# Order of the three split products: term by term across output tiles, with FFN gate and up chunks in pairs (two-block transformer, one Trainium2 core)

## Chip, core and metric

The program runs on 1 core of one Trainium2 chip. The metric is device time in microseconds (us), the median of several executions. The engines are TensorE (PE, matrix products; its weight load is listed as PEld), VectorE (DVE), ScalarE (ACT), GpSimd (POOL, nearly unused here) and SyncE (SP, which issues the weight loads).

## What is computed

Two transformer blocks of two layers each over 256 tokens of width 1024, all inputs and outputs float32. The parts that the change touches are dense products: the projections of the mixers (qkv, output, cross-attention and memory projections), and the feed-forward part (FFN) of the first block:

```python
def conv_ffn(x, w_gate, w_up, conv_w, conv_b, w_down):
    gt = x @ w_gate
    gt = lax.conv_general_dilated(
        gt, conv_w[:, None, :].astype(gt.dtype), window_strides=(1,),
        padding=[(CONV_WIDTH - 1, 0)], dimension_numbers=('NWC', 'WIO', 'NWC'),
        feature_group_count=gt.shape[-1]) + conv_b
    return (jax.nn.silu(gt) * (x @ w_up)) @ w_down
```

Gate and up go from 1024 to 2816 features; the convolution has three taps along the tokens.

The same program also holds attention, an RWKV-7 mixer, sparse latent attention and two mixtures of experts; the change touches none of their own products.

## The kernel before

**Split products.** Each float32 operand of a touched product is split into a high part (a cast to `fp32r`, by ACT, line 510) and a low part (the operand less its high part, by DVE, line 513). `three` (line 515) adds three products for one output tile and one block of 128 rows: high by high, high by low, low by high. Each is one PE instruction at line 518.

```python
for n, (x, y) in enumerate(((0, 0), (0, 1), (1, 0))):
    last = pe.matmul(out, a[x], b[y], start=start and n == 0, stop=stop and n == 2, skip_group_check=True)
```

PSUM is used as 8 banks of 512 columns (`bank(b)`). There are three callers of `three`.

- `project` (line 609): a unit is 512 output columns; its 8 chunks are the 8 blocks of 128 rows. For each chunk PE makes the three products for token tile 0 in one bank and then for token tile 1 in the next, 512 columns wide.
- `project_features` (line 678): the same weight chunks, the output transposed: four tiles of 256 columns, two to a bank, visited in the order m = 0, 1, 2, 3.
- `ffn_stage` (line 896), called once for each of the first block's two layers (n_units = FU = 11).

**The FFN stage.** A unit u is 256 hidden features. Its weights (3 MB) come by one DMA into a ring of four slots. It has six chunks of 128x1024 weights: c = 0, 1 are the two gate tiles, c = 2, 3 the two up tiles, c = 4, 5 the two halves of the down product. `order` is the list of chunks in which PE, ACT and DVE take them: unit u's four gate and up chunks, then chunks 4 and 5 of unit u - 1. `number` is a chunk's place in it. The split weights lie in `bufs = 4` buffers, so chunk q may be cast once chunk q - 4 has been used. The gate tiles of unit u are two halves of bank 2(u mod 2), the up tiles of bank 2(u mod 2) + 1; the down products add up in banks 4 to 7.

Per gate or up chunk PE makes 8 x 3 products of 256 columns, per down chunk 4 x 3 products of 512. After the last product of a chunk PE raises `used` ("chunk_used") by one. What the other engines do within a unit is written out by hand, in this order:

ACT, unit u:

1. casts of the unit's four gate and up chunks (`split_chunk`, line 960);
2. `wait_used(act, u, 1)`: both gate tiles are there;
3. two activations (line 989), conv = gate times the last tap plus bias, which raise `biased`;
4. casts of unit u - 1's chunks 4 and 5;
5. wait for `conv_ready`, Silu (line 996), wait for `hid_made`, cast of the hidden tile.

DVE, unit u:

1. low parts of the four chunks (line 1007, 513);
2. wait for `biased`, then four convolution steps (line 1028) that read the gate bank;
3. low parts of unit u - 1's chunks 4 and 5;
4. `wait_used(dve, u, 3)`, then the product with the up tiles (line 1039);
5. the hidden tile's low part, which raises `hidden_ready`.

Unit u's down chunks need `hidden_ready` of unit u; they come one unit later. In unit 0 there are no down chunks, and what follows the hidden tile on ACT and DVE is the split of unit 1's chunks. After the last unit ACT and DVE only split the down chunks that are left. In the second layer ACT also issues six DMAs at the start of unit 1 (line 978).

Of the kernel before, what the change touches and what calls it, by code (L numbers as in the profile page):

```python
# [88 lines left out]
def build_program(nc, d, out):  # L89
    with ExitStack() as ctx:  # L90
# [424 lines left out]
        def three(pe, out, a, b, start, stop):  # L515
# [2 lines left out]
                last = pe.matmul(out, a[x], b[y], start=start and n == 0, stop=stop and n == 2, skip_group_check=True)  # L518
            return last

        @contextmanager
        def split_operands(bufs, width):

            close_part()
            with ExitStack() as space:
                opened[0] += 1
                yield [[space.enter_context(nc.sbuf_tensor(f"{name}_{x}{opened[0]}", shape, F32R))[:] for x in "hl"]
                       for name, shape in (("x", [P, KD, SEQ]), ("w", [P, bufs, width]))]
            open_part()
# [79 lines left out]
        def project(units, dest=None, src=None, rotary=None, residual=None, row_src=(), loads_due=None, norm=None):  # L609


            src = xT if src is None else src
            j0 = next_unit(units)
            with split_operands(BUFS, COLS) as (xs, ws), new_block() as block:
                used, evac, free = sig("chunk_used"), sig("act_evacuated"), sig("dve_evacuated")
                rows_in = sig("rows_loaded")

                @block.tensor
                def _(pe):
                    if norm is None:  # L620
                        fill(pe, 5)
                    else:
                        fill(pe, 3, 0)
                        norm_pe(pe, norm, split_place, SPLIT_AFTER)
                        fill(pe, 2, 0)
                    for q in range(KD * units):
                        u, k = q // KD, q % KD
                        chunk_ready(pe, q, norm)
                        if u >= 2 and k == 0:
                            if residual is None:  # L630
                                pe.wait_ge(evac.sem, evac.at(T * (u - 1)))
                            else:
                                pe.wait_ge(free.sem, free.at(T * (u - 1)))
                        for t in range(T):
                            last = three(pe, bank(T * (u % 2) + t), [x[:, k, t * P:(t + 1) * P] for x in xs], [w[:, q % BUFS, :] for w in ws], k == 0, k == KD - 1)
                        last.then_inc(used.up(), 1)
                    if residual is not None:
                        fill(pe, 5)

                def load_rows(act):  # L640
                    for i, r in enumerate(row_src):
                        act.dma_start(rows[:, i, :], r.rearrange("(o f) -> o f", o=1).broadcast_to([P, D])).then_inc(rows_in.up(16), 16)

                def act_evac(act, u):
                    if residual is not None and u == units - 1:
                        load_root(act)
                    if residual is None:
                        act.wait_ge(used.sem, used.at(KD * (u + 1)))
                        for t in range(T):
                            act.copy(dest(u, t), bank(T * (u % 2) + t)).then_inc(evac.up(), 1)  # L650

                def dve_evac(dve, u):
                    if residual is not None:
                        dve.wait_ge(used.sem, used.at(KD * (u + 1)))
                        for t in range(T):
                            add_residual(dve, t, u, residual, bank(T * (u % 2) + t)).then_inc(free.up(), 1)
                    elif rotary is not None and rotary(u) is not None:
                        heads, dh, at, rot, cos, sin, tmp = rotary(u)
                        for t in range(T):
                            dve.wait_ge(evac.sem, evac.at(T * u + t + 1))  # L660
                            link(dve, "dve_step", rope(dve, dest(u, t), heads, dh, at, rot, cos[:, t, :], sin[:, t, :], tmp))

                split_projection(block, j0, units, src, xs, ws, act_evac, dve_evac, act_first=load_rows, norm=norm)
                stream(block, units if loads_due is None else loads_due)
# [13 lines left out]
        def project_features(src, dst, units=2, act_aside=None, dve_aside=None, norm=None):  # L678

            j0 = next_unit(units)  # L680
            with split_operands(BUFS, COLS) as (xs, ws), new_block() as block:
                used, evac = sig("chunk_used"), sig("act_evacuated")

                @block.tensor
                def _(pe):
                    if norm is None:
                        fill(pe, 5)
                    else:
                        fill(pe, 3, 0)
                        norm_pe(pe, norm, split_place, SPLIT_AFTER)  # L690
                        fill(pe, 2, 0)
                    for q in range(KD * units):
                        u, k = q // KD, q % KD
                        chunk_ready(pe, q, norm)
                        if u >= 2 and k == 0:
                            pe.wait_ge(evac.sem, evac.at(2 * (u - 1)))
                        for m in range(4):
                            last = three(pe, bank(2 * (u % 2) + m // 2)[:, (m % 2) * SEQ:(m % 2 + 1) * SEQ], [w[:, q % BUFS, m * P:(m + 1) * P] for w in ws],
                                         [x[:, k, :] for x in xs], k == 0 and m % 2 == 0, k == KD - 1)
                        last.then_inc(used.up(), 1)  # L700

                def act_evac(act, u):
                    act.wait_ge(used.sem, used.at(KD * (u + 1)))
                    for n in range(2):
                        o = dst[:, 4 * u + 2 * n:4 * u + 2 * n + 2, :]
                        act.copy(o, bank(2 * (u % 2) + n).rearrange("p (m s) -> p m s", m=2)).then_inc(evac.up(), 1)

                def on_the_side(dve):
                    if dve_aside is not None:
                        dve_aside(dve)  # L710
                    scale_rows(dve)

                split_projection(block, j0, units, src, xs, ws, act_evac, lambda dve, u: None, act_between=act_aside, dve_between=on_the_side, norm=norm)
                stream(block, units)
# [181 lines left out]
        def ffn_stage(n_units, layer, norm, row_src=(), ahead=()):  # L896
# [5 lines left out]
            with ExitStack() as space:  # L902
# [5 lines left out]

                order = []
                for u in range(n_units + 1):  # L910
                    order += [(u, c) for c in range(4) if u < n_units] + [(u - 1, c) for c in (4, 5) if u]
                number = {x: q for q, x in enumerate(order)}

                def source(u, c):
# [9 lines left out]
                with new_block() as block:  # L924
# [9 lines left out]
                    def _(pe):  # L934
                        fill(pe, 3, 0)
                        norm_pe(pe, norm, split_place, SPLIT_AFTER)
                        fill(pe, 4, 0)
                        for u, c in order:
                            pe.wait_ge(split.sem, split.at(number[u, c] + 1))
                            w = [chunk(part, u, c) for part in range(2)]  # L940
                            if c < 4:
                                if c == 0 and u >= 2:
                                    pe.wait_ge(hid_ready.sem, hid_ready.at(u - 1))
                                for k in range(KD):
                                    if number[u, c] == 0:
                                        pe.wait_ge(x_ready.sem, x_ready.at(k + 1))
                                    mm = three(pe, bank(2 * (u % 2) + c // 2)[:, (c % 2) * SEQ:(c % 2 + 1) * SEQ], [x[:, k, :] for x in w], [x[:, k, :] for x in xs],
                                               k == 0, k == KD - 1)
                            else:
                                pe.wait_ge(hid_ready.sem, hid_ready.at(u + 1))  # L950
                                for t in range(T):
                                    for n in range(2):
                                        mm = three(pe, bank(4 + 2 * t + n), [x[:, u % 2, c - 4, t * P:(t + 1) * P] for x in hids], [x[:, n * 512:(n + 1) * 512] for x in w],
                                                   u == 0 and c == 4, u == n_units - 1 and c == 5)
                            mm.then_inc(used.up(), 1)
                        fill(pe, 9, 0)

                    @block.scalar
                    def _(act):
# [14 lines left out]
                        for u in range(n_units + 1):  # L974
# [2 lines left out]
                                for o, x in ahead:  # L977
                                    act.dma_start(o, x).then_inc(ahead_in.up(16), 16)
                            if u < n_units:
                                for c in range(4):  # L980
                                    if u or c:
                                        split_chunk(u, c)
                                wait_used(act, u, 1)
# [22 lines left out]
                    def _(dve):  # L1006
# [8 lines left out]
                        for u in range(n_units + 1):  # L1015
                            b = u % 2
                            if u < n_units:
                                for c in range(4):
                                    if u or c:
                                        split_chunk(u, c)  # L1020
                                gt = bank(2 * b).rearrange("p (f s) -> p f s", f=2)
# [1447 lines left out]
```

## Time and profile before

| | |
|---|---|
| median of 3 runs | 1984.71 us (1984.04 to 1984.95) |
| span of the profiled execution, first to last instruction | 1976.8 us |
| median less that span (what lies around it) | 7.9 us |
| PE busy / PEld busy | 1830.9 us (93%) / 1418.6 us (72%) |
| DVE busy / ACT busy | 935.1 us (47%) / 727.1 us (37%) |
| mean granted TensorE clock | 0.972 of full speed |
| data moved | 374.36 MB, 189 GB/s mean |

The page lists the span of the profiled execution and no other time of it, so the 7.9 us is the difference to the median of the runs. The FFN stages lie at about 171 to 364 us and 690 to 890 us of the span. A matmul's duration in the trace is longer than the distance to the next one's start, as successive matmuls overlap; the distance between starts ("pitch" below) is what a product costs in a row of them. PE's idle time before an instruction stands in square brackets in the timeline, counted from the end of the product before.

### The profile page before, as it was taken

How to read it: one execution, taken by the hardware profiler on the slowest of the kernel's cores; microseconds unless marked ns; L12 is line 12 of the kernel's file. 1: busy time of each engine (PE TensorE's matmuls, PEld its weight loads, DVE VectorE, ACT ScalarE, POOL GpSimd, SP SyncE). 2: the span in 40 equal slices, each digit the busy share in tenths (PEclk: the TensorE clock that was granted, in tenths of full speed). 3: DMA queues.
4: the chain of work that ended last, by engine and by line, in shares of the span. 5: the costliest groups of instructions: out<-in, count | busy, mean ns of one | idle time of the engine just before them, and what ended most of it. 6: DMA issues, size and time to landing. Idle time of an engine off the chain costs nothing. (4 is left out here: it accounts for less than half of the span.)

```text
span 1976.8 us, 31147 instructions
## 1 busy us (share of the span) xinstructions
PE 1830.9 (93%) x13140; PEld 1418.6 (72%) x13140; DVE 935.1 (47%) x1881; ACT 727.1 (37%) x1341; POOL 0.2 (0%) x4
## 2 busy tenths in 40 slices
PE   7998999999999789998999989999988898899997
PEld 6778999785798589997777777555544677755553
DVE  6565566512766655656557656111123665611012
ACT  4465444203343354444545543111122454411111
POOL 0000000000000000000000000000000000000000
PEclk9999999999899799999999998999998999999998
DMA  7503443242000434442450333999972133399994
GB/s 292 213 1 128 192 192 150 88 181 112 23 3 3 191 106 192 192 151 71 162 207 7 107 150 132 410 426 423 426 298 86 43 107 149 132 377 423 425 424 181
DMA packets 33983, 374.36 MB, mean 189 GB/s; under 512 B 4896, under 2 KB 6048, under 8 KB 9264
## 3 DMA queue, kind: packets, MB, share of 16 engines
q1 hardware_dynamic: 30688, 363.89, 46.3%
q10 hardware_dynamic: 3152, 8.42, 1.2%
q8 instruction: 107, 1.75, 0.4%
q14 instruction: 36, 0.29, 0.0%
HBM read 371.25 MB, written 1.05 MB: 188 GB/s over the span
## 5 line engine op out<-in xcount | busy, mean ns | idle before, releaser
L1870 PE MATMUL ps<-ring,arena 128*64 128x256 f32 x2048 | 235.1, 382 | 0.0
L510 ACT CAST w_h<-ring 128x512 fp32r<-128x512 f32 x256 | 156.9, 622 | 155.4 <-PE ps L518 138.0
L148 PE MATMUL ps<-ident 128*128 128x256 f32 x652 | 171.4, 406 | 45.0 <-PEq L827 8.1
L513 DVE TENSOR_TENSOR w_l<-ring,w_h 128x512 fp32r<-128x512 f32 x256 | 172.0, 690 | 85.4 <-ACT w_h L510 83.2
L518 PE MATMUL ps<-ffn_x_h,ffn_w_h 128*128 128x256 f32 x704 | 201.3, 286 | 10.2 <-DVE ffn_w_l L513 10.0
L518 PE MATMUL ps<-ffn_x_l,ffn_w_h 128*128 128x256 f32 x704 | 200.6, 285 | 0.0
L518 PE MATMUL ps<-ffn_x_h,ffn_w_l 128*128 128x256 f32 x704 | 200.4, 285 | 0.0
L1870 PEld LDWEIGHTS ps<-ring,arena 128*64 128x64 f32 x2048 | 141.4, 137 | 69.1
L148 PEld LDWEIGHTS ps<-ident 128*128 128x128 f32 x652 | 124.5, 202 | 71.9 <-issue 56.7
L518 PE MATMUL ps<-w_h,x_h 128*128 128x512 f32 x416 | 164.1, 395 | 5.5 <-DVE w_l L513 5.5
L513 DVE TENSOR_TENSOR ffn_w_l<-ring,ffn_w_h 128x1024 fp32r<-128x1024 f32 x132 | 155.5, 1221 | 22.3 <-ACT ffn_w_h L510 22.3
L518 PE MATMUL ps<-w_h,x_l 128*128 128x512 f32 x416 | 162.2, 390 | 0.0
L518 PE MATMUL ps<-w_l,x_h 128*128 128x512 f32 x416 | 162.2, 390 | 0.0
L510 ACT CAST ffn_w_h<-ring 128x1024 fp32r<-128x1024 f32 x132 | 131.3, 1045 | 39.7 <-PE ps L518 23.0
L518 PEld LDWEIGHTS ps<-ffn_x_h,ffn_w_h 128*128 128x128 f32 x704 | 136.4, 194 | 11.7 <-DVE ffn_w_l L513 11.0
L518 PEld LDWEIGHTS ps<-ffn_x_l,ffn_w_h 128*128 128x128 f32 x704 | 136.4, 194 | 0.8
L518 PEld LDWEIGHTS ps<-ffn_x_h,ffn_w_l 128*128 128x128 f32 x704 | 136.5, 194 | 0.0
L2101 DVE TENSOR_TENSOR arena<-arena,ps 64x256 f32<-64x256 f32 x64 | 27.2, 425 | 225.4 <-ACT arena L1986 225.3
L1986 ACT ACTIVATE arena<-ps 64x256 f32<-64x256 f32 x64 | 24.1, 376 | 272.7 <-PE ps L1870 272.7
L1891 PE MATMUL ps<-ring,routing 128*64 128x512 f32 x512 | 122.3, 598 | 0.8 <-DVE routing L2103 0.8
L2103 DVE COPY routing<-ps 128x128 f32<-128x128 f32 x64 | 18.7, 292 | 170.8 <-PE ps L1922 170.8
L518 PEld LDWEIGHTS ps<-w_h,x_h 128*128 128x128 f32 x416 | 78.4, 188 | 25.0 <-DVE w_l L513 5.1
(343 smaller groups left out, 2966.4 us busy)
## 6 DMA issues: line engine op xcount, KB each, us to landing
ring<-in_w_moe SPq DMA_DIRECT2D x64, 2048.0 KB, 11.1
ring<-in_w_proj SPq DMA_DIRECT2D x38, 2048.0 KB, 8.2
ring<-in_w_ffn SPq DMA_DIRECT2D x22, 3072.0 KB, 10.5
ring<-in_w_moe SPq DMA_DIRECT2D x64, 1024.0 KB, 11.4
rows<-in_ln_g ACTq DMA_DIRECT2D x6, 512.0 KB, 3.9
rows<-in_ln_b ACTq DMA_DIRECT2D x6, 512.0 KB, 5.3
ring<-in_w_lora SPq DMA_DIRECT2D x1, 2560.0 KB, 9.1
ring<-in_w_b_in SPq DMA_DIRECT2D x1, 2496.0 KB, 9.8
```

Of the source, the lines that this page charges most:

```text
L148: pe.matmul(bank(b)[:, 0:2 * P].rearrange("p (o f) -> p o f", o=2), ident[:], wide, start=True, stop=True, skip_group_check=True)
L510: act.copy(high, x).then_inc(ready.up(), 1)
L513: return dve.tensor_tensor(low, x, high.bitcast(F32), ALU.subtract)
L518: last = pe.matmul(out, a[x], b[y], start=start and n == 0, stop=stop and n == 2, skip_group_check=True)
L1870: last = pe.matmul(bank(0)[g * SLOTS_E:(g + 1) * SLOTS_E, 0:2 * P], x[:, k, e * SLOTS_E:(e + 1) * SLOTS_E], wg[:, g, k, :], start=(k == 0) ...
L1891: last = pe.matmul(bank(2)[c * SLOTS_E:(c + 1) * SLOTS_E, :], hids[:, f, :], wd[:, f, c * 512:(c + 1) * 512], start=(n % 2 == 0 and f == 0 ...
L1986: act.activation(sg[SLOTS_E:2 * SLOTS_E, :], bank(0)[0:SLOTS_E, 0:2 * P], ACT.Silu).then_inc(silu_done.up(), 1)
L2101: dve.tensor_tensor(hid_tok[up, :], sg[up, :], bank(0)[up, 0:2 * P], ALU.mult).then_inc(hid_made.up(), 1)
L2103: dve.tensor_copy(hids, bank(1)[:, 0:2 * SLOTS_E].rearrange("p (f s) -> p f s", f=2)).then_inc(hid_ready.up(), 1)
```

## The change

A second helper makes the same products for several output tiles at once: term by term, and within a term tile by tile. `project` and the down product use it with the two tiles of a chunk. `project_features` uses it with its four tiles in the order m = 0, 2, 1, 3. In the FFN, PE takes a gate chunk and an up chunk together: (u, 0) with (u, 2), then (u, 1) with (u, 3). It waits for both splits, makes 8 x 3 x 2 products that alternate between the gate bank and the up bank, and raises `used` by two after the last. `order` becomes 0, 2, 1, 3 for the gate and up chunks, on ACT and DVE too. Number of buffers, number of products, and the waits and order of everything else on ACT and DVE stay as they are; `wait_used(act, u, 1)` is still the wait before the two activations.

```diff
+        def three_each(pe, jobs, begin, stop):
+
+            for n, (x, y) in enumerate(((0, 0), (0, 1), (1, 0))):
+                for out, a, b, opens in jobs:
+                    last = pe.matmul(out, a[x], b[y], start=begin and opens and n == 0, stop=stop and n == 2, skip_group_check=True)
+            return last
...
@@ project
-                        for t in range(T):
-                            last = three(pe, bank(T * (u % 2) + t), [x[:, k, t * P:(t + 1) * P] for x in xs], [w[:, q % BUFS, :] for w in ws], k == 0, k == KD - 1)
-                        last.then_inc(used.up(), 1)
+                        tiles = [(bank(T * (u % 2) + t), [x[:, k, t * P:(t + 1) * P] for x in xs], [w[:, q % BUFS, :] for w in ws], True) for t in range(T)]
+                        three_each(pe, tiles, k == 0, k == KD - 1).then_inc(used.up(), 1)
...
@@ project_features
-                        for m in range(4):
-                            last = three(pe, bank(2 * (u % 2) + m // 2)[:, (m % 2) * SEQ:(m % 2 + 1) * SEQ], [w[:, q % BUFS, m * P:(m + 1) * P] for w in ws],
-                                         [x[:, k, :] for x in xs], k == 0 and m % 2 == 0, k == KD - 1)
-                        last.then_inc(used.up(), 1)
+                        tiles = [(bank(2 * (u % 2) + m // 2)[:, (m % 2) * SEQ:(m % 2 + 1) * SEQ], [w[:, q % BUFS, m * P:(m + 1) * P] for w in ws],
+                                  [x[:, k, :] for x in xs], m % 2 == 0) for m in (0, 2, 1, 3)]
+                        three_each(pe, tiles, k == 0, k == KD - 1).then_inc(used.up(), 1)
...
@@ ffn_stage
-                    order += [(u, c) for c in range(4) if u < n_units] + [(u - 1, c) for c in (4, 5) if u]
+                    order += [(u, c) for c in (0, 2, 1, 3) if u < n_units] + [(u - 1, c) for c in (4, 5) if u]
...
                         for u, c in order:
+                            if c in (2, 3):
+                                continue
                             pe.wait_ge(split.sem, split.at(number[u, c] + 1))
-                            if c < 4:
+                            if c < 2:
+                                pe.wait_ge(split.sem, split.at(number[u, c + 2] + 1))
...
-                                    mm = three(pe, bank(2 * (u % 2) + c // 2)[:, (c % 2) * SEQ:(c % 2 + 1) * SEQ], [x[:, k, :] for x in w], [x[:, k, :] for x in xs],
-                                               k == 0, k == KD - 1)
+                                    tiles = [(bank(2 * (u % 2) + g)[:, c * SEQ:(c + 1) * SEQ], [chunk(part, u, 2 * g + c)[:, k, :] for part in range(2)], [x[:, k, :] for x in xs], True)
+                                             for g in range(2)]
+                                    mm = three_each(pe, tiles, k == 0, k == KD - 1)
+                                mm.then_inc(used.up(2), 2)
...
-                                for c in range(4):
+                                for c in (0, 2, 1, 3):
```

PE in the FFN stage, from a unit's first product to its first down product (`ffn_w` is the split weight, `ffn_x` the split input, `ffn_hid` the split hidden tile, `_h` and `_l` the high and low parts). Before:

```order
L518 MATMUL ps<-ffn_x_h,ffn_w_h 128x256 [waits hidden_ready,weights_split]
L518 MATMUL ps<-ffn_x_l,ffn_w_h 128x256
L518 MATMUL ps<-ffn_x_h,ffn_w_l 128x256
...
L518 MATMUL ps<-ffn_x_h,ffn_w_h 128x256 [waits weights_split]
...
L518 MATMUL ps<-ffn_w_h,ffn_hid_h 128x512 [waits hidden_ready,weights_split]
L518 MATMUL ps<-ffn_w_l,ffn_hid_h 128x512
L518 MATMUL ps<-ffn_w_h,ffn_hid_l 128x512
```

and with the change:

```order
L525 MATMUL ps<-ffn_x_h,ffn_w_h 128x256 [waits hidden_ready,weights_split]
L525 MATMUL ps<-ffn_x_h,ffn_w_h 128x256
L525 MATMUL ps<-ffn_x_l,ffn_w_h 128x256 x2
L525 MATMUL ps<-ffn_x_h,ffn_w_l 128x256 x2
...
L525 MATMUL ps<-ffn_x_h,ffn_w_h 128x256 [waits weights_split]
...
L525 MATMUL ps<-ffn_w_h,ffn_hid_h 128x512 [waits hidden_ready,weights_split]
L525 MATMUL ps<-ffn_w_h,ffn_hid_h 128x512
L525 MATMUL ps<-ffn_w_l,ffn_hid_h 128x512 x2
L525 MATMUL ps<-ffn_w_h,ffn_hid_l 128x512 x2
```

Every term now stands twice in a row, once for each bank. The row that waits for weights alone stands three times in a unit before (chunks 1, 2 and 3) and once now (the second pair).

ACT in the FFN stage, one whole unit. Before:

```order
L510 CAST ffn_w_h<-ring 128x1024 [waits chunk_used,weights_loaded2]
L510 CAST ffn_w_h<-ring 128x1024 [waits chunk_used] x3
L989 ACTIVATE arena_0<-ps,cols 128x256 [waits hidden_ready,chunk_used]
L989 ACTIVATE arena_0<-ps,cols 128x256
L510 CAST ffn_w_h<-ring 128x1024 [waits chunk_used] x2
L996 ACTIVATE arena_0<-arena_0 128x512 [waits conv_ready]
L510 CAST ffn_hid_h<-arena_0 128x512 [waits chunk_used,hidden_made]
```

and with the change:

```order
L510 CAST ffn_w_h<-ring 128x1024 [waits chunk_used,weights_loaded2]
L510 CAST ffn_w_h<-ring 128x1024 [waits chunk_used] x3
L998 ACTIVATE arena_0<-ps,cols 128x256 [waits hidden_ready,chunk_used]
L998 ACTIVATE arena_0<-ps,cols 128x256
L510 CAST ffn_w_h<-ring 128x1024 [waits chunk_used] x2
L1005 ACTIVATE arena_0<-arena_0 128x512 [waits conv_ready]
L510 CAST ffn_hid_h<-arena_0 128x512 [waits chunk_used,hidden_made]
```

Nothing has moved but line numbers: the two activations on the gate tiles still stand ahead of the casts of the two down chunks. DVE's rows are the same too (its convolution steps now have line 1037, its product with the up tiles line 1048).

## Rows read from the trace of the kernel before

**Rows 1.** The page, part 1: busy time, share and instructions of each engine.
```profile
PE 1830.9 (93%) x13140; PEld 1418.6 (72%) x13140; DVE 935.1 (47%) x1881; ACT 727.1 (37%) x1341; POOL 0.2 (0%) x4
```
**Rows 2.** Groups by line: out<-in, shape, xcount | busy us, mean ns | idle before.
```profile
L518 PE MATMUL ps<-ffn_x_h,ffn_w_h 128*128 128x256 f32 x704 | 201.3, 286 | 10.2 <-DVE ffn_w_l L513 10.0
...
L518 PE MATMUL ps<-w_h,x_h 128*128 128x512 f32 x416 | 164.1, 395 | 5.5 <-DVE w_l L513 5.5
...
L518 PE MATMUL ps<-ffn_w_h,ffn_hid_h 128*128 128x512 f32 x176 | 68.7, 390 | 0.0
...
L518 PE MATMUL ps<-x_h,w_h 128*128 128x256 f32 x192 | 56.4, 294 | 10.8 <-DVE w_l L513 10.8
```
**Rows 3.** Timeline of PE, last up product and first down products of a unit: start us, duration us.
```profile
302.42 0.28 PE L518 MATMUL ps<-ffn_x_h,ffn_w_l 128*128 128x256 f32 x1
302.54 0.40 PE L518 MATMUL ps<-ffn_w_h,ffn_hid_h 128*128 128x512 f32 x1
302.77 0.40 PE L518 MATMUL ps<-ffn_w_l,ffn_hid_h 128*128 128x512 f32 x1
303.01 0.39 PE L518 MATMUL ps<-ffn_w_h,ffn_hid_l 128*128 128x512 f32 x1
303.23 0.40 PE L518 MATMUL ps<-ffn_w_h,ffn_hid_h 128*128 128x512 f32 x1
```
**Rows 4.** Timeline of ACT: the two activations on the gate tiles, two units in succession.
```profile
229.06 1.02 ACT L989 ACTIVATE arena<-ps,cols 128x256 f32<-128x256 f32 x2 [4.71 <-PE ps L518]
...
246.04 1.02 ACT L989 ACTIVATE arena<-ps,cols 128x256 f32<-128x256 f32 x2 [4.71 <-PE ps L518]
```
**Rows 5.** Timeline of PE: last product of the second gate chunk, and the next.
```profile
245.72 0.28 PE L518 MATMUL ps<-ffn_x_h,ffn_w_l 128*128 128x256 f32 x1
245.84 0.28 PE L518 MATMUL ps<-ffn_x_h,ffn_w_h 128*128 128x256 f32 x1
```
**Rows 6.** Timeline of DVE in the unit of the first of rows 4.
```profile
230.11 1.78 DVE L1028 SCALAR_TENSOR_TENSOR arena<-ps,cols,arena 128x255 f32<-128x255 f32 x4 [4.50 <-ACT arena L989]
231.81 2.35 DVE L513 TENSOR_TENSOR ffn_w_l<-ring,ffn_w_h 128x1024 fp32r<-128x1024 f32 x2
234.82 0.69 DVE L1039 TENSOR_TENSOR arena<-arena,ps 128x512 f32<-128x512 f32 x1 [0.65 <-PE ps L518]
...
237.15 3.50 DVE L513 TENSOR_TENSOR ffn_w_l<-ring,ffn_w_h 128x1024 fp32r<-128x1024 f32 x3 [0.26 <-ACT ffn_w_h L510]
```
**Rows 7.** Start of the first FFN stage: DVE's splits of chunks 1 to 3, and PE.
```profile
173.75 3.50 DVE L513 TENSOR_TENSOR ffn_w_l<-ring,ffn_w_h 128x1024 fp32r<-128x1024 f32 x3 [0.45 <-ACT ffn_w_h L510]
...
175.03 0.39 PE L518 MATMUL ps<-ffn_x_h,ffn_w_h 128*128 128x256 f32 x1
```
**Rows 8.** End of unit 0 of the first FFN stage, ACT, DVE and PE.
```profile
178.20 1.02 ACT L989 ACTIVATE arena<-ps,cols 128x256 f32<-128x256 f32 x2 [2.59 <-PE ps L518]
...
181.07 0.63 ACT L996 ACTIVATE arena<-arena 128x512 f32<-128x512 f32 x1 [0.55 <-DVE arena L1028]
...
183.95 0.69 DVE L1039 TENSOR_TENSOR arena<-arena,ps 128x512 f32<-128x512 f32 x1 [2.92 <-PE ps L518]
...
187.55 0.39 PE L518 MATMUL ps<-ffn_x_h,ffn_w_h 128*128 128x256 f32 x1 [3.64 <-DVE ffn_w_l L513]
```
**Rows 9.** The same point of the second FFN stage, PE.
```profile
714.05 0.58 PE L518 MATMUL ps<-ffn_x_h,ffn_w_h 128*128 128x256 f32 x1 [6.32 <-DVE ffn_w_l L513]
```
**Rows 10.** PE in stretches around those waits: stretch, length, busy us (x products), granted clock, DMA.
```profile
188.30:191.50 3.20, 3.20 (x16) 0.50 0.00 0
...
710.50:717.10 6.60, 3.05 (x14) 0.50 0.68 213
...
1136.60:1143.00 6.40, 4.06 (x34) 1.00 0.91 342
```
**Rows 11.** Timeline of PE, a wait in `project_features` inside the last stretch of rows 10.
```profile
1141.67 0.39 PE L518 MATMUL ps<-x_h,w_h 128*128 128x256 f32 x1 [2.34 <-DVE w_l L513]
```
**Rows 12.** Groups by line: the expert products, two at a time in halves of the array.
```profile
L1870 PE MATMUL ps<-ring,arena 128*64 128x256 f32 x2048 | 235.1, 382 | 0.0
```

More of the change, by code:

```diff
@@ L938, in _ @@
                         for u, c in order:
+                            if c in (2, 3):
+                                continue
                             pe.wait_ge(split.sem, split.at(number[u, c] + 1))
-                            w = [chunk(part, u, c) for part in range(2)]
-                            if c < 4:
+                            if c < 2:
+                                pe.wait_ge(split.sem, split.at(number[u, c + 2] + 1))
                                 if c == 0 and u >= 2:
@@ L946, in _ @@
                                         pe.wait_ge(x_ready.sem, x_ready.at(k + 1))
-                                    mm = three(pe, bank(2 * (u % 2) + c // 2)[:, (c % 2) * SEQ:(c % 2 + 1) * SEQ], [x[:, k, :] for x in w], [x[:, k, :] for x in xs],
-                                               k == 0, k == KD - 1)
+                                    tiles = [(bank(2 * (u % 2) + g)[:, c * SEQ:(c + 1) * SEQ], [chunk(part, u, 2 * g + c)[:, k, :] for part in range(2)], [x[:, k, :] for x in xs], True)
+                                             for g in range(2)]
+                                    mm = three_each(pe, tiles, k == 0, k == KD - 1)
+                                mm.then_inc(used.up(2), 2)
                             else:
+                                w = [chunk(part, u, c) for part in range(2)]
                                 pe.wait_ge(hid_ready.sem, hid_ready.at(u + 1))
                                 for t in range(T):
[L952 to L955, printed above, removed]
+                                    tiles = [(bank(4 + 2 * t + n), [x[:, u % 2, c - 4, t * P:(t + 1) * P] for x in hids], [x[:, n * 512:(n + 1) * 512] for x in w], True) for n in range(2)]
+                                    mm = three_each(pe, tiles, u == 0 and c == 4, u == n_units - 1 and c == 5)
+                                mm.then_inc(used.up(), 1)
                         fill(pe, 9, 0)
@@ L1017, in _ @@
                             if u < n_units:
-                                for c in range(4):
+                                for c in (0, 2, 1, 3):
                                     if u or c:
```

## The prediction

> **What bounds the kernel now.** The page's busy line comes first: PE is busy 93% of the span, DVE 47%, ACT 37% [rows 1]. So PE's row of instructions is the path, and the change can act in two ways: by the distance between PE's products, or by what PE waits for. The groups by line give the number of products that are reordered [rows 2]; each row is one of three terms. 256 columns wide: 3 x 704 in the FFN and 3 x 192 in `project_features`, 2688 in all. 512 wide: 3 x 416 in `project` and 3 x 176 down products, 1776. Together 4464.
>
> Next the timeline of PE for the pitch. A 256-wide product is followed by the next after 0.12 us (245.72 to 245.84) [rows 5], a 512-wide one after 0.23 (302.54 to 303.23, 0.69 in three steps) [rows 3]. A unit of the FFN has 96 of the first and 24 of the second, and the activations on the gate tiles return after 246.04 - 229.06 = 16.98 us [rows 4]: less 96 x 0.120, 5.46 are left for 24, which is 0.2275 each, the pitch of rows 3. So a steady unit holds products end to end and no wait of PE; the stage is bound by PE's pitch. In the whole run PE waits for FFN weights for 10.0 us only [rows 2], 3.64 in the first stage and 6.32 in the second, both at unit 1's first chunk [rows 8, 9].
>
> **Part 1, the order across banks.** Would a change of bank shorten the pitch? The old order already holds such steps. From the last up product to the first down product the bank changes: 302.42 to 302.54, 0.12, the same as within a bank. In the down product the third term is followed by the first of another bank: 303.01 to 303.23, 0.22, against 0.23 and 0.24 for the two steps within a bank, which is the rounding of the timeline [rows 3]. So I take 0 for all 4464. The bounds: 256 columns more cost 0.107 us (0.227 - 0.120), so of the 0.120 only 0.013 doesn't belong to the columns. If alternation removed all of it, 4464 x 0.013 = 58 us would go; that is the lower end. For the upper end 1 ns each, 4 us. I take 0, since the measured steps across banks are the nearest rows there can be. `project` and `project_features` keep their waits, buffers and counts, so nothing else changes there.
>
> **Part 2, the gate tiles come late.** This is the term that decides. ACT may read the gate bank when both gate chunks are used. Today that is after chunks 0 and 1: the activations start at 246.04, 0.04 after the last gate product's end at 246.00 [rows 4, 5], while PE works on the two up chunks for another 48 x 0.120 = 5.76 us. That is the cover of all that follows: activations, convolution, split of the down chunks. With the change the second gate chunk shares a pair with the second up chunk, and `used` rises by two at that pair's end: ACT's wait for place 2 of the unit isn't met by the first pair. The cover is gone. Behind the waiting activations stand, on ACT, the casts of both down chunks, and on DVE, behind the convolution that waits for the activations, their low parts. PE wants those next.
>
> Count from the end of the pair's last product. Activations start at 0.04. DVE's first low part of a down chunk starts 231.81 - 229.06 = 2.75 after them [rows 4, 6], at 2.79; it takes 1.22 (two in 2.35, so 1.13 or 1.14 from one to the next [rows 6]), and PE starts 0.06 after such an end (173.75 + 1.22 = 174.97, start 175.03 [rows 7]). PE restarts at 4.07. The last product's end lies 0.28 - 0.12 = 0.16 after the moment at which the next could have started [rows 5], so **4.23 us are lost**. Buffers aren't the cause: both down chunks go where the first pair has been.
>
> What is late next: DVE ends the second down chunk at 2.79 + 2.35 = 5.14 and starts the product with the up tiles at 5.16; from there to its first split of the next unit it is 237.15 - 234.82 = 2.33 [rows 6], so 7.49. PE now needs two chunks before it starts: 7.49 + 1.14 + 1.22 + 0.06 = 9.91. PE is done with the down chunks at 4.07 + 24 x 0.227 = 9.52. **0.4 us more.** The second pair's splits follow within 2.4 us, under the first pair's 5.76. Ten units of a stage (1 to 10) have the first loss, nine the second (none follows unit 10): 42.3 + 3.6 = 45.9 us.
>
> Unit 0 has no down chunks; there the next unit's chunks stand behind the whole chain. Silu starts 181.07 - 178.20 = 2.87 after the activations and takes 0.63, so it ends at 3.54 and the product with the up tiles starts at 3.58. From that product to PE's restart it is 187.55 - 183.95 = 3.60 today [rows 8], and 1.13 more because the pair needs both splits: 8.31, against the 3.64 of today. **4.7 us more**; in the second stage, where ACT issues DMAs inside this chain in both kernels, 4.7 on top of the 6.32 [rows 9].
>
> The stage's start: PE begins today with one split chunk while the other three are split, and the second starts at 175.03 [rows 7]. The pair can start only there. One chunk of 24 x 0.120 = **2.9 us** is lost. At the stage's end nothing: the last hidden tile is ready at 5.16 + 0.69 + the cast and the low part, some 7.2, and needed at 9.5.
>
> Per stage 45.9 + 4.7 + 2.9 = 53.5, for both **+107 us**. The weight DMAs need less speed than before, and the ring stays full.
>
> A rule of the Trainium skill speaks to this place. Perfetto Trace Analysis, section Optimizing Tensor Performance (Matmuls), says that independent groups of matmuls should rotate through PSUM banks so that the evacuation of one overlaps the products of the next. Read for this change, what counts is a group that is finished while another one runs, and not alternation itself. The trace agrees: the gate's evacuation runs today under the up products [rows 4, 5]. By alternation alone as a benefit the sum would be 0 or less; by the rows it is +107.
>
> **Part 3, the clock.** After the 3.64 us wait PE worked 3.2 us at a granted clock of 0.50 (1.2 GHz), after the 6.32 us wait 3.05 us within a stretch of 6.6; with a wait of 2.34 us the clock stayed at 1.00 (2.4 GHz) [rows 8 to 11]. The new waits of 4 us lie above the one that cost a fall. At 0.50 the trace has 16 products of 256 columns in 3.2 us [rows 10]; at 0.120 each they would take 1.9, so 3.2 us at the low level lose 1.3. There are 12 waits of about 4 us or more in a stage (start, and the ends of units 0 to 10), 24 in all: 24 x 1.3 = 31, less the two falls that exist (2.6), about **+29 us**. Bounds: no new fall, 0; each wait keeps PE low for a whole 6.6 us of work, 2.7 each, 24 x 2.7 - 2.6 = 62.
>
> **Sum.** 0 + 107 + 29 = 136 us on a span of 1976.8, 2112.8. The runs' median stands 7.9 above that span, so **2121 us**, 7% slower.
>
> **Rivals.**
>
> *The clock holds.* 1984.7 + 107 = 2092. For it: the waits are part of a 21 us period in which PE is otherwise busy. Against: the falls after 3.64 and 6.32. 0.15.
>
> *The clock stays low longer.* 1984.7 + 107 + 62 = 2154. For it: the fall after 6.32 lasted 6.6 us. Against: the new waits are shorter. 0.07.
>
> *The fixed part of the pitch goes.* If 0.013 us of every product is a delay that the alternation avoids, 58 us come back: 2121 - 58 = 2063. Against it stand rows 3. 0.13. The Trainium skill gives a pitch beside it (TensorE: Matmul & The Clock Gate, section Back-to-back issue gap): columns divided by 2.4 GHz plus 2.5 ns, 109.2 ns for 256 columns and 215.8 for 512, whatever the bank. The trace shows 120 and 227 instead. If the new order reached the page's figures, 2688 x 0.0108 + 1776 x 0.0112 = 49 us would come back, an estimate of 2072 us.
>
> *Faster: products in different banks overlap.* The expert products run two at a time in halves of the array: 235.1 us for 2048, 0.115 each [rows 12]. If two products in different banks ran half over each other, 2688 x 0.060 + 1776 x 0.113 = 362 us would go, for some 1760. It decides from a saving of 136 / 4464 = 0.030 us a product on, more than twice the fixed part. Against: both products want the whole array (128*128 in rows 3), and a step across banks shows nothing of it. 0.03.
>
> *The late gate doesn't hold PE.* If the activations were released by the first pair, or the down chunks were split ahead of them, part 2 would shrink to the start and the double waits, some 10 us; only if these were hidden too would the time be the same. The ACT order stands ahead of me and says no. 0.02 for no difference.
>
> **How the numbers follow.** Forecast 0.60, with its own range of 2102 to 2140 (the falls' 29 us could be half or one and a half times that, 15 either way, and 1 ns of pitch is 4). From 2060, which takes in the rival of the fixed part, to 2150 the range holds the forecast, the clock that holds, and the fixed part; left out are the long falls and the last two, 0.12 in all, and whatever I haven't seen. 0.2% (4 us) is about what a measurement of this kernel can tell from no change. Faster 0.03, same 0.02, slower 0.95.
>
> **What would show it.** Right: in both FFN stages ACT's activations start 0.04 us after the end of an up and gate pair; PE waits some 4.1 us for DVE's low part at each first down chunk, 20 times, and 0.2 to 0.4 at each next pair; the activations return after about 21.6 us plus what the clock takes; PE's idle time for FFN weights goes from 10 to about 110 us; a dozen or more stretches at 0.50 in each stage. The pitch stays 0.120 and 0.227. Wrong: a pitch below 0.12 anywhere in line 525, activations that start in the middle of a unit, or waits without falls of the clock.

## The result, and the profile after

The changed kernel takes **2131.82 us** (median of 4 runs, 2131.53 to 2135.26) against 1984.38 for the kernel before beside it (4 runs, 1979.81 to 1984.95). The ratio is 1.0751, with a 95% interval of 1.0734 to 1.0768: 147 us slower. Forecast was 2121, in a range of 2060 to 2150.

The page, part 1, and from part 5 the two groups of FFN products that answer to the first and third of [rows 2] (out<-in, shape, xcount | busy us, mean ns | idle before):

```profile
PE 1893.9 (89%) x13140; PEld 1464.4 (69%) x13140; DVE 934.8 (44%) x1881; ACT 728.0 (34%) x1341; POOL 0.2 (0%) x4
...
L525 PE MATMUL ps<-ffn_x_h,ffn_w_h 128*128 128x256 f32 x704 | 145.2, 289 | 25.6 <-DVE ffn_w_l L513 25.6
...
L525 PE MATMUL ps<-ffn_w_h,ffn_hid_h 128*128 128x512 f32 x176 | 76.0, 522 | 81.2 <-DVE ffn_w_l L513 81.2
```

Three readings. The instruction counts are those of [rows 1], and ACT's and DVE's busy times are the same to 1 us: nothing was added or removed. The first group's busy time fell from 201.3 to 145.2 us, and that is no gain: a group's busy time counts overlapping instructions once, and the same term now stands twice in a row, so each pair overlaps within its own group. The mean of one, 289 ns against 286, says that a product is what it was. And the down products' mean rose from 390 to 522 ns, with 81.2 us of idle time before them where there was none: a wait and a slow clock at this place.

Who waited for whom on PE (us in total, times, longest), first rows:

```profile
PE ps L525 <- DVE ffn_w_l L513: 106.7, 24, 11.1
PE ps L525 <- DVE w_l L513: 16.3, 11, 6.2
```

The wait for the FFN's split weights was 10.0 us in all [rows 2] and is 106.7. The 24 times are the two stage starts, unit 1 of each stage, and the first down chunk of 20 units. The other waits are the old ones.

PE's timeline around one of the twenty, then ACT's activations on the gate tiles (start us, us of one, engine, line, operation, out<-in, shape, how many, and in brackets the idle time before and what ended it):

```profile
234.91 0.40 PE L525 MATMUL ps<-ffn_x_l,ffn_w_h 128*128 128x256 f32 x2
235.15 0.40 PE L525 MATMUL ps<-ffn_x_h,ffn_w_l 128*128 128x256 f32 x2
239.60 1.22 PE L525 MATMUL ps<-ffn_w_h,ffn_hid_h 128*128 128x512 f32 x2 [4.06 <-DVE ffn_w_l L513]
```

```profile
235.58 1.02 ACT L998 ACTIVATE arena<-ps,cols 128x256 f32<-128x256 f32 x2 [10.46 <-PE ps L525]
...
354.56 1.02 ACT L998 ACTIVATE arena<-ps,cols 128x256 f32<-128x256 f32 x2 [10.46 <-PE ps L525]
...
378.44 1.02 ACT L998 ACTIVATE arena<-ps,cols 128x256 f32<-128x256 f32 x2 [10.46 <-PE ps L525]
```

The last products end at 235.15 + 0.40 = 235.55, ACT starts at 235.58, and PE waits 4.06 us for DVE. DVE in the same unit does what the prediction counted, in the order of [rows 6]:

```profile
236.63 1.78 DVE L1037 SCALAR_TENSOR_TENSOR arena<-ps,cols,arena 128x255 f32<-128x255 f32 x4 [10.26 <-ACT arena L998]
238.33 2.35 DVE L513 TENSOR_TENSOR ffn_w_l<-ring,ffn_w_h 128x1024 fp32r<-128x1024 f32 x2
240.60 0.68 DVE L1048 TENSOR_TENSOR arena<-arena,ps 128x512 f32<-128x512 f32 x1
```

A unit now takes 378.44 - 354.56 = 23.88 us, against 16.98 [rows 4]. Of the 6.90 more, 4.23 are the wait. The rest, 2.67, is the clock: the unit's 24 down products take from 358.58 to the next pair's start at 366.73, 8.15 us for 5.45 at the pitch of [rows 3]. PE in three stretches of this unit (stretch, length, busy us (x products), granted clock, DMA share, GB/s): the wait, the work behind it, and the work after that.

```profile
354.60:358.50 3.90, 0.00 (x0) 0.85 0.00 0
358.70:364.00 5.30, 5.30 (x13) 0.50 0.62 223
364.20:378.40 14.20, 14.20 (x108) 1.00 0.30 127
```

The level falls inside the wait and stays at 0.50 (1.2 GHz) through 5.3 us of work. In that stretch PE makes 13 down products where a pitch of 0.227 would give some 23.

PE over the two stages of the kernel before:

```profile
171.00:365.00 194.00, 190.27 (x1328) 0.99 0.41 157
695.00:891.00 196.00, 189.56 (x1326) 0.98 0.44 164
```

And of the changed kernel:

```profile
175.00:444.00 269.00, 219.05 (x1321) 0.85 0.30 114
780.00:1048.00 268.00, 215.88 (x1320) 0.86 0.32 120
```

About 75 and 72 us longer each, together the 147 us by which the medians differ; the mean clock fell from 0.99 and 0.98 to 0.85 and 0.86. (The two profiled spans, 1976.8 and 2133.5 us, are 157 us apart. The 10 us left over lie outside the stages and within what the kernel before itself varies by from run to run, 1978 to 1989 us.) The pitch did not change: in the timeline above two pairs of products start 0.24 us apart (234.91, 235.15), 0.120 a product, now across banks at every step.

### The profile page after: what moved, and what is told of

Same layout as the page of the kernel before. It is cut to its first block and busy times, and to the rows that moved or that the text cites. A ratio compares the mean times of both kernels' runs of the same rounds, so it can differ in the third digit from the quotient of the medians.

```text
span 2133.5 us, 31171 instructions
## 1 busy us (share of the span) xinstructions
PE 1893.9 (89%) x13140; PEld 1464.4 (69%) x13140; DVE 934.8 (44%) x1881; ACT 728.0 (34%) x1341; POOL 0.2 (0%) x4
## 5 line engine op out<-in xcount | busy, mean ns | idle before, releaser
L525 PE MATMUL ps<-ffn_x_h,ffn_w_h 128*128 128x256 f32 x704 | 145.2, 289 | 25.6 <-DVE ffn_w_l L513 25.6
L525 PE MATMUL ps<-ffn_w_h,ffn_hid_h 128*128 128x512 f32 x176 | 76.0, 522 | 81.2 <-DVE ffn_w_l L513 81.2
L525 PE MATMUL ps<-ffn_x_l,ffn_w_h 128*128 128x256 f32 x704 | 144.6, 288 | 0.0
L525 PE MATMUL ps<-ffn_x_h,ffn_w_l 128*128 128x256 f32 x704 | 144.3, 287 | 0.0
L1037 DVE SCALAR_TENSOR_TENSOR arena<-ps,cols,arena 128x255 f32<-128x255 f32 (+1 forms) x88 | 38.4, 478 | 235.2 <-ACT arena L998 234.4
L525 PE MATMUL ps<-w_h,x_h 128*128 128x512 f32 x416 | 130.1, 394 | 5.5 <-DVE w_l L513 5.5
L525 PE MATMUL ps<-w_l,x_h 128*128 128x512 f32 x416 | 128.3, 389 | 0.0
L525 PE MATMUL ps<-w_h,x_l 128*128 128x512 f32 x416 | 128.1, 389 | 0.0
L525 PEld LDWEIGHTS ps<-ffn_x_l,ffn_w_h 128*128 128x128 f32 x704 | 112.7, 197 | 0.0
L525 PEld LDWEIGHTS ps<-ffn_x_h,ffn_w_l 128*128 128x128 f32 x704 | 112.5, 197 | 0.0
```

Source lines behind the costliest of these rows:

```text
L525: last = pe.matmul(out, a[x], b[y], start=begin and opens and n == 0, stop=stop and n == 2, skip_group_check=True)
L1037: ins = dve.scalar_tensor_tensor(x, gt[:, f, 0:SEQ - lag], col("conv_w", (layer * 3 + w) * FT + ft), x, ALU.mult, ALU.add)
```

## The experiments

The first four ran beside each other on one chip, with the kernel before at 1982.63 us (17 runs, 1978.48 to 1989.08); the last three beside the kernel before at 1983.26 (11 runs, 1978.53 to 1989.31). The changed kernel was not run again beside them; where its 2131.82 us are compared with an experiment, the kernel before differs by 1 to 2 us between the two sides.

### The new orders without the pairs (e1_orders_only)

The FFN's gate and up chunks as before, everything else as changed.

```diff
-                    order += [(u, c) for c in (0, 2, 1, 3) if u < n_units] + [(u - 1, c) for c in (4, 5) if u]
+                    order += [(u, c) for c in range(4) if u < n_units] + [(u - 1, c) for c in (4, 5) if u]
...
-                                    mm = three_each(pe, tiles, k == 0, k == KD - 1)
-                                mm.then_inc(used.up(2), 2)
+                                    mm = three(pe, bank(2 * (u % 2) + c // 2)[:, (c % 2) * SEQ:(c % 2 + 1) * SEQ], [x[:, k, :] for x in w], [x[:, k, :] for x in xs],
+                                               k == 0, k == KD - 1)
+                                mm.then_inc(used.up(), 1)
```

> The term-by-term order across banks is kept in the projections, the transposed projections and the down product; the FFN's gate and up chunks are taken one by one again, as before. Theory (the gate's late release holds PE, the order itself costs and gives nothing): 1984 us, within 4. Rival 1 (the order itself gains the fixed 13 ns of each reordered product, 1776 + 576 products here): 1954 us. Rival 2 (part of the 147 us comes from the new order): 2000 us or more.

Measured: 1984.03 us (12 runs, 1980.8 to 1990.47), ratio 1.0005 (0.9994 to 1.0017). The order across banks gains nothing and costs nothing, to within 0.2%, for the 2352 products of the projections and the down product; for the FFN's gate and up products the 0.120 us in the changed kernel's timeline says it. The timeline of a projection shows why:

```profile
39.98 0.62 PE L525 MATMUL ps<-w_l,x_h 128*128 128x512 f32 x2
40.44 0.61 PE L525 MATMUL ps<-w_h,x_l 128*128 128x512 f32 x2
40.89 0.62 PE L525 MATMUL ps<-w_h,x_h 128*128 128x512 f32 x2
41.34 0.62 PE L525 MATMUL ps<-w_l,x_h 128*128 128x512 f32 x2
```

The four rows start 0.46, 0.45 and 0.45 us apart, two products each; six products from 39.98 to 41.34 are 1.36 us, 0.227 each: the pitch of the old order [rows 3], with a change of bank at every step. The rival in which the fixed 13 ns go, and with it the estimate of 2072 us from the Trainium skill's gap, is out. (That section, Back-to-back issue gap in TensorE: Matmul & The Clock Gate, gives its formula for an isolated product. The products here come in a stream, each with a weight load [rows 1].)

### The late gate alone (e2_late_gate)

The kernel before, with one number changed.

```diff
-                                wait_used(act, u, 1)
+                                wait_used(act, u, 3)
```

> The kernel before with one number changed: ACT's wait ahead of the two gate activations asks for the fourth chunk of the unit (second up chunk) in place of the second. No pairs, no new order. Theory (late release alone makes the time): PE waits 4.06 us at each first down chunk, 20 times, and 7.2 us at unit 1 of each stage; 10 x 4.23 + 3.5 = 46 us a stage, 92 for both, and for the clock some 36 us as in the changed kernel (147 - 107 = 40 there for 24 waits): 2112 us. Rival (pairs starve PE through four buffers): no more than 1990 us.

Measured: 2123.48 us (2121.79 to 2125.68), ratio 1.071 (1.0693 to 1.0728). One number costs 141 us, where the whole change costs 147, with no pair and no new order; the two stage starts that only the pairs lose, 2 x 2.9 us, are about the rest. The waits are where they were expected, 22 times and 98.3 us in all, and their length is the same. Its waits of PE (us in total, times, longest):

```profile
PE ps L518 <- DVE ffn_w_l L513: 98.3, 22, 9.9
```

PE's timeline of this kernel in one of these units:

```profile
302.43 0.80 PE L518 MATMUL ps<-ffn_w_h,ffn_hid_h 128*128 128x512 f32 x1 [4.06 <-DVE ffn_w_l L513]
```

The time is 11 us above what I had put on record, since I had taken 36 us for the clock there; by the same account it was 49 (2123.5 - 1982.6 - 92).

### Pairs of the same kind (e3_same_kind_pairs)

```diff
-                            if c in (2, 3):
+                            if c in (1, 3):
                                 continue
...
-                                pe.wait_ge(split.sem, split.at(number[u, c + 2] + 1))
+                                pe.wait_ge(split.sem, split.at(number[u, c + 1] + 1))
...
-                                    tiles = [(bank(2 * (u % 2) + g)[:, c * SEQ:(c + 1) * SEQ], [chunk(part, u, 2 * g + c)[:, k, :] for part in range(2)], [x[:, k, :] for x in xs], True)
+                                    tiles = [(bank(2 * (u % 2) + c // 2)[:, g * SEQ:(g + 1) * SEQ], [chunk(part, u, c + g)[:, k, :] for part in range(2)], [x[:, k, :] for x in xs], g == 0)
```

with `range(4)` as the order of the chunks on all three engines.

> The changed kernel with other pairs: both gate chunks together, then both up chunks, alternating between the two halves of one bank. Pairs, the wait for two splits and the raise by two stay. Theory: the activations start under the up pair again, so the 4 us waits go; what stays is one chunk at the stage's start (2.9 us) and 1.1 us at unit 1, 8 us for both stages, and up to two more falls of the clock: 1990 to 1997 us. Rival (pairing as such costs): 2100 us or more.

Measured: 1995.48 us (1989.45 to 1998.08), ratio 1.007 (1.0053 to 1.0086), as expected. Pairing, with its double wait and its double raise on four buffers, costs 13 us, at the stage's start and at unit 1: 18.4 us of waits where the kernel before has 10.0, and two more falls of the clock in the two stages.

```profile
PE ps L525 <- DVE ffn_w_l L513: 18.4, 4, 7.5
```

In a steady unit it costs nothing, if the pair leaves a pair behind it to cover the gate's evacuation:

```profile
218.53 1.02 ACT L998 ACTIVATE arena<-ps,cols 128x256 f32<-128x256 f32 x2 [4.71 <-PE ps L525]
235.51 1.02 ACT L998 ACTIVATE arena<-ps,cols 128x256 f32<-128x256 f32 x2 [4.71 <-PE ps L525]
```

These are ACT's activations of two units in a row (timeline): 235.51 - 218.53 = 16.98 us, the old unit.

### The waits filled, first try (e4_filled_waits)

The changed kernel with idle products where PE waits, to see what the time is if its clock does not fall.

```diff
-                        fill(pe, 4, 0)
+                        fill(pe, 16, 0)
...
+                            if (u, c) == (1, 0):
+                                fill(pe, 36, 2)
+                            if c == 4 and u < n_units - 1:
+                                pe.wait_ge(hid_ready.sem, hid_ready.at(u + 1))
+                                fill(pe, 17, 2 * (u % 2))
```

> The changed kernel with idle products on the identity (256 columns, 0.216 us each at the full clock) put where PE waits: 12 more at the stage's start, 36 ahead of unit 1, 17 ahead of each first down chunk that is waited for. The waits themselves stay. It measures the clock's share by itself. Theory: the clock stays at 1.00 in both FFN stages, ACT and DVE are untouched, and the time is 1984 + 107, 2091 us (2085 to 2095). Rival (the clock's falls hide under the waits or the fills only move them): 2125 us or more.

Measured: 2154.57 us (2152.29 to 2157.32), ratio 1.0869 (1.085 to 1.0887). The experiment was mis-sized, and its time says nothing on the question. A fill is two instructions, not one, so each block lasts nearly twice the wait:

```profile
240.59 7.50 PE L148 MATMUL ps<-ident 128*128 128x256 f32 x34
```

### The waits filled to size (e5_fitted_fills)

The same with 10 for 16, 19 for 36, and 9 for 17 (the first number is that of the stage's start).

> As e4_filled_waits, with the count mended: one fill is two PE instructions of 0.216 us, so the fills there were twice as long as the waits (7.5 us against 4.1) and held PE up themselves. Here 9 fills (3.9 us) ahead of each first down chunk that is waited for, 19 (8.2 us) ahead of unit 1, 6 more (2.6 us) at the stage's start. Theory: the clock stays at 1.00 in both FFN stages, a steady unit takes 16.98 + 4.23 + 0.4 = 21.6 us, and the time is 1983 + 107 = 2090 us (2085 to 2097); the clock's share of the 147 us is then about 40. Rival (the falls cost little by themselves): 2120 us or more.

Measured: 2086.02 us (2083.83 to 2087.52), ratio 1.0518 (1.0495 to 1.0541). The granted clock in the two stages:

```profile
174.00:416.00 242.00, 239.14 (x1540) 1.00 0.32 123
753.00:999.00 246.00, 240.54 (x1540) 0.99 0.34 127
```

ACT's activations return after 21.58 us, where 21.6 had been worked out:

```profile
249.70 1.02 ACT L1003 ACTIVATE arena<-ps,cols 128x256 f32<-128x256 f32 x2 [10.77 <-PE ps L525]
271.29 1.02 ACT L1003 ACTIVATE arena<-ps,cols 128x256 f32<-128x256 f32 x2 [10.77 <-PE ps L525]
```

The fills do not hold PE up themselves: at all 24 places it still waits for DVE's low part at their end, 7.4 us in all. One fall is left, in the second stage, behind the 2.8 us by which unit 1's wait outlasts its fills.

This splits the loss. The waits cost 2086.0 - 1983.3 = 103 us, the falls of the clock 2131.8 - 2086.0 = 46 us. The kernel computes what the changed one does; the fills' products are overwritten.

### The down chunks split first (e6_down_first)

ACT and DVE take the two down chunks ahead of the gate.

```diff
+                                if u:
+                                    for c in (4, 5):
+                                        split_chunk(u - 1, c)
                                 wait_used(act, u, 1)
...
-                            if u:
+                            if u == n_units:
                                 for c in (4, 5):
                                     split_chunk(u - 1, c)
```

and the same on DVE, ahead of its wait for `biased`.

> The changed kernel with ACT and DVE splitting the two down chunks of unit u - 1 ahead of the gate's activations and convolution, not behind them. Pairs and the late gate stay. Theory: what holds PE is not the late gate but what stands behind it. The 4.06 us wait at the first down chunk goes; the next unit's pair, now the first thing behind the chain, is ready 8.3 us after the pair's end and PE is done with the down chunks after 5.3, so 3.0 us are lost a unit instead of 4.6: 27 + 7.6 = 35 us a stage, 2053 us if the clock holds, up to 2090 with a fall in each unit. Rival (the new waits come from the buffers, not from the order on ACT and DVE): 2125 us or more.

Measured: 2094.55 us (2087.07 to 2097.56), ratio 1.0552 (1.0523 to 1.0581). The wait left the down chunk and came back in front of the next pair, with the length that was expected:

```profile
258.47 0.61 PE L525 MATMUL ps<-ffn_w_h,ffn_hid_l 128*128 128x512 f32 x2
262.04 0.77 PE L525 MATMUL ps<-ffn_x_h,ffn_w_h 128*128 128x256 f32 x2 [2.96 <-DVE ffn_w_l L513]
```

So the place of the wait follows the order on ACT and DVE, and not the buffers. The clock's mean is 0.88 and 0.89 in the two stages, and it is low behind the wait above, so waits of 2.96 us bring falls as well. The time is just past the upper end of what was expected, 2090 us. PE behind that wait and in the two stages (the same columns as above):

```profile
262.10:266.70 4.60, 4.60 (x22) 0.50 0.00 0
...
175.00:424.00 249.00, 211.33 (x1320) 0.88 0.32 122
759.00:1008.00 249.00, 209.29 (x1322) 0.89 0.34 128
```

### The same mechanism used the other way (e7_early_unit1)

The kernel before waits at one place for what stands behind the hidden tile's chain: unit 1's first chunk [rows 8, 9]. Here ACT and DVE split unit 1's gate chunks earlier, and in the second stage ACT's six DMA issues move one unit later (the first lines below).

```diff
-                            if u == 1:
+                            if u == 2:
                                 for o, x in ahead:
...
-                                    if u or c:
+                                    if (u or c) and (u, c) not in ((1, 0), (1, 1)):
                                         split_chunk(u, c)
...
+                            if u == 0:
+                                for c in (0, 1):
+                                    split_chunk(1, c)
```

The last two blocks stand on ACT behind the activations, and on DVE behind the convolution.

> The kernel before, with the same mechanism used the other way at the one place where it waits: in unit 0 ACT and DVE split unit 1's two gate chunks right behind the activations and the convolution, ahead of the hidden tile's chain, and the second stage's six DMA issues on ACT move from unit 1 to unit 2. Theory: the waits of 3.64 and 6.32 us at unit 1 go, and the two falls of the clock behind them (1.5 us each): 13 us less, 1970 us, 0.6% faster than before. Rival (the wait only moves to the next chunks): within 4 us of before.

Measured: 1971.84 us (6 runs, 1967.58 to 1973.16), ratio 0.9934 (0.9916 to 0.9952): 0.7% below the kernel before, as expected, and clear of no change. The waits of 3.64 and 6.32 us are gone, 0.8 us of waiting for FFN weights is left in the whole run (before unit 2 of the second stage, where the DMA issues now stand), and neither stage has a fall of the clock. In the first stage, where ACT issues no DMA here, the earlier splits alone take the wait away; in the second the two edits were not tried apart. Its group of gate and up products:

```profile
L518 PE MATMUL ps<-ffn_x_h,ffn_w_h 128*128 128x256 f32 x704 | 199.8, 284 | 1.0 <-DVE ffn_w_l L513 0.8
```

PE in the two stages of this kernel (columns as for the stages above):

```profile
171.00:359.00 188.00, 187.92 (x1326) 1.00 0.42 160
696.00:886.00 190.00, 189.04 (x1330) 1.00 0.45 171
```

## Why the prediction was right, and where it was off

- **The order across banks: 0 us.** Right. 1.0005 with an interval of 0.0023 (e1), the pitch at 0.227 and 0.120 with a bank change at every step. It could be read from the old trace, because its order changed banks at every third down product already.
- **The late gate: 4.23 us for each of 20 units.** Right to 0.01: 4.06 us of idle time where 4.07 had been worked out. That one waiting instruction is the cause is shown by e2 (the wait alone, 141 us), e3 (pairs without it, 13 us) and e6 (the wait moves with the order behind it).
- **The second wait of 0.4 us a unit.** Off in the changed kernel, where it never appears: at all 18 places the next pair starts 0.45 or 0.46 us after the last two down products, which is their pitch. The step took the down products at the full clock, 5.45 us; behind the wait they run mostly at 0.50 and take 8.2, so both splits are there in time. With the clock held (e5) the next pair starts 0.64 to 0.69 us after them, and the unit takes 21.58 us, 0.37 more than 16.98 + 4.23. So the step was right for a clock that holds, and the low clock hides the wait. It is 7 us over both stages. PE at this place, in the changed kernel and in e5:

```profile
366.28 0.62 PE L525 MATMUL ps<-ffn_w_h,ffn_hid_l 128*128 128x512 f32 x2
366.73 0.40 PE L525 MATMUL ps<-ffn_x_h,ffn_w_h 128*128 128x256 f32 x2
...
258.81 0.61 PE L525 MATMUL ps<-ffn_w_h,ffn_hid_l 128*128 128x512 f32 x2
259.50 0.47 PE L525 MATMUL ps<-ffn_x_h,ffn_w_h 128*128 128x256 f32 x2
```

- **Unit 1 and the stage's start: 4.7 and 2.9 us.** Right: 8.31 us were worked out for unit 1 of the first stage, and the trace has 8.47; the second stage has 11.06, for 6.32 + 4.7. At the two starts PE waits 3.00 and 3.03 us, for 2.9.

The row for unit 1 of the first stage in the changed kernel, PE:

```profile
197.61 0.77 PE L525 MATMUL ps<-ffn_x_h,ffn_w_h 128*128 128x256 f32 x2 [8.47 <-DVE ffn_w_l L513]
```

- **The clock: 29 us.** This is the term that was mis-sized; it measures 46 against e5. The step put 1.3 us on a fall, from 3.2 us of work at the low level. In the changed kernel the granted clock falls 12 times in each stage, once for each wait, the two starts of 3.0 us among them. The low level mostly holds through 5.3 us of work, as in the unit above, and costs 2.67 us there, of which 0.37 are the second wait that it hides. Over the 24 waits the mean is 1.9 us. The true price lay between the value taken and the upper bound (2.7), which had been read from the second of the old falls [rows 10].
- **The sum.** Predicted 0 + 107 + 29 = 136; by e5 it is 0 + 103 + 46 = 149 against that job's kernel before. The 29 had the kernel before's own two falls taken off (2.6 us by the prediction's price), and the 46 has not. On the prediction's footing the split is 105 + 43: 2 us under on the waits, 14 over on the clock. The 14 us lie just inside the 15 that the forecast allowed the clock either way.
- **The 7.9 us between span and median** were no property of the program. The profiled execution after has a span of 2133.5 us and a time of its own of 2135.26, 1.8 apart. With the same 1.8 the profiled execution before took 1978.6, and other runs of that kernel took 1978.48 to 1989.08. Where the profile's own time isn't listed, the difference between span and median holds the scatter of the runs too.

The rule that groups should rotate through banks so that the evacuation of one overlaps the products of the next (the Trainium skill, Perfetto Trace Analysis, section Optimizing Tensor Performance) holds here in its second half. e1 rotates more and gains nothing. e3 alternates within one bank only and keeps the overlap, and loses 13 us; the changed kernel alternates between two banks and loses the overlap, and 147.

## What to carry to other kernels

When tiles are produced together, they are also finished together: ask what was done with the first one while the second was made, and list what stands behind that work on its engines. Before reordering products for a gain in pitch, look for the same step in the old order; here every third product answered the question. And cost a new wait on TensorE twice, for its length and for the products behind it that run at half clock.

## What the runs showed of the hardware that I had not expected

- The steady unit of the changed kernel and of e2_late_gate have the same length, 23.9 us, though e2 needs no second chunk before a unit starts (e2: activations at 298.41 and 322.31): the second wait of the changed kernel is hidden. In the first stage of the changed kernel the last ten falls begin 23.9 us apart, and the units' length settles at that distance (23.51, 23.69, 23.75, 23.84 and on to 23.90).

```profile
298.41 1.02 ACT L989 ACTIVATE arena<-ps,cols 128x256 f32<-128x256 f32 x2 [10.46 <-PE ps L518]
...
322.31 1.02 ACT L989 ACTIVATE arena<-ps,cols 128x256 f32<-128x256 f32 x2 [10.46 <-PE ps L518]
```

- Waits of 2.96 us that return every 20 to 23 us are enough for the clock to fall at most of them (e6): 15 of the 18 units that end in one take 21.7 to 22.9 us, and the other three 20.2, which is 16.98 and the wait, without a fall. A single wait of 2.34 us was not enough [rows 10, 11].
- Idle products on the identity hold the clock at 1.00 through waits of 4 us, and give back 46 us in a kernel that waits 24 times (e5). In the changed kernel that is still 5% slower than not waiting at all.
